# A two-block transformer on one core: five of eight modulation loads move from the ring to GpSimd's queue, and two orders in the expert mixtures change

## The reference

```
def first_block(x, c, ada_w, ada_b, norm1_g, norm2_g, even_w_in, even_w_out, ...):
    c_act = jax.nn.silu(c)
    for layer in range(DEPTH):
        mod = (c_act @ ada_w[layer] + ada_b[layer])[:, None, :]
        sh1, sc1, g1, sh2, sc2, g2 = jnp.split(mod, 6, axis=-1)
        h = rms_norm(x, norm1_g[layer]) * (1.0 + sc1) + sh1
        if layer % 2 == 0:
            mix = even_mixer(h, even_w_in[i], even_w_out[i], ...)
        else:
            mix = odd_mixer(h, odd_w_in[i], odd_w_out[i])
        x = x + g1 * mix
        h = rms_norm(x, norm2_g[layer]) * (1.0 + sc2) + sh2
        x = x + g2 * grouped_moe(h, router_w, router_b, exp_w_gate[layer], exp_w_up[layer], exp_w_down[layer])
    return x
```

## Time and profile before

| | us |
|---|---|
| median of 3 runs | 2006.47 |
| lowest, highest | 2000.43, 2013.55 |
| the profiled execution | 2012.27 |
| its span | 2010.2 |
| TensorE busy in it | 1887.3 |
| VectorE busy | 1182.9 |
| ScalarE busy | 944.8 |

### The profile page before, as it was taken

The page is one execution under the profiler, slowest core; times in us unless marked ns, Lnnn a source line. Parts: engine busy times, 40 slices in busy tenths (PEclk is TensorE's granted clock), DMA queues, the critical chain, the costliest instruction groups (busy, mean ns, idle before and its releaser), DMA issues.

```text
span 2010.2 us, 32548 instructions
## 1 busy us (share of the span) xinstructions
PE 1887.3 (94%) x13756; PEld 1388.2 (69%) x13756; DVE 1182.9 (59%) x1634; ACT 944.8 (47%) x1346; POOL 72.2 (4%) x126
## 2 busy tenths in 40 slices
PE   7988998899988988999999999899999999899998
PEld 4776623246975342358889877788888888778887
DVE  5878733446877433556666744666665676536665
ACT  3445444446463544464446633354455454545443
POOL 1040000000110000000000000000000000200000
PEclk9989997999998979999999989999999999999999
DMA  9876899997956899975555200345545555505552
GB/s 372 331 250 256 332 416 390 421 421 282 343 159 278 356 388 421 420 296 202 189 189 178 92 24 4 146 170 189 188 160 203 193 188 189 153 19 192 189 189 105
DMA packets 69216, 476.42 MB, mean 237 GB/s; under 512 B 8512, under 2 KB 8576, under 8 KB 13776
## 3 DMA queue, kind: packets, MB, share of 16 engines
q1 hardware_dynamic: 60592, 437.32, 57.0%
q0 software_dynamic: 8480, 37.03, 5.6%
HBM read 472.17 MB, written 2.14 MB: 236 GB/s over the span
## 4 chain that ended last, share of the span: by engine, by line
PE 74%; DMA 9%; DVE 9%; ACT 5%; issue 3%; SPq 0%; POOL 0%; DVEq 0%; ACTq 0%; POOLq 0%
PE psum L1160 16%; PE psum L1195 11%; PE psum L1608 11%; PE psum L1165 8%; DMA experts<-in_exp_blocks 6%; PE psum L1115 4%; PE psum L1550 1%; DVE w_lo L3102 1%; PE psum L1128 1%; PE psum L1623 1%; PE psum L1129 1%; PE psum L1130 1%; DMA pool<-in_ada_w 1%; ACT w_hi L2331 1%; PE psum L1064 1%
## 5 line engine op out<-in xcount | busy, mean ns | idle before, releaser
L3102 DVE TENSOR_TENSOR w_lo<-ring,w_hi 128x2048 fp32r<-128x2048 f32 x191 | 436.9, 2293 | 183.9 <-ACT w_hi L2331 182.4
L2331 ACT ACTIVATE w_hi<-ring 128x2048 fp32r<-128x2048 f32 x191 | 365.1, 1915 | 203.6 <-PE psum L1195 117.9
L1160 PE MATMUL psum<-h_both,w_hi 128*128 128x512 f32 x1408 | 442.5, 395 | 1.9 <-DVE h_both L3888 1.3
L1165 PEld LDWEIGHTS psum<-h_both,w_lo 128*128 128x128 f32 x1408 | 264.5, 188 | 61.8
L1165 PE MATMUL psum<-h_both,w_lo 128*128 128x256 f32 x1408 | 277.2, 278 | 0.0
L2540 ACT ACTIVATE pool<-experts 128x512 f32 x332 | 183.8, 622 | 186.2 <-PE psum L1608 115.5
L3546 DVE COPY pool<-experts 128x512 f32 x380 | 141.4, 423 | 201.9 <-PE psum L1608 129.1
L1160 PEld LDWEIGHTS psum<-h_both,w_hi 128*128 128x128 f32 x1408 | 217.3, 189 | 5.7 <-issue 1.7
L2363 ACT ACTIVATE pool<-psum 128x512 f32<-128x512 f32 x88 | 52.7, 598 | 254.3 <-PE psum L1165 254.3
L1608 PE MATMUL psum<-pool 128*32 128x512 f32 x1008 | 123.2, 604 | 12.9 <-DVE pool L3546 11.5
L1608 PE MATMUL psum<-experts,pool 128*32 128x512 f32 x1024 | 122.5, 613 | 3.7 <-DMA experts<-in_exp_blocks 1.9
(11 more groups left out here) (508 smaller groups left out, 3004.3 us busy)
## 6 DMA issues: line engine op xcount, KB each, us to landing
ring<-in_weight_pieces SPq DMA_DIRECT2D x193, 1024.0 KB, 4.8
experts<-in_exp_blocks SPq DMA_DIRECT2D x192, 1024.0 KB, 15.4
ring<-in_ada_w SPq DMA_DIRECT2D x24, 1024.0 KB, 6.0
pool<-in_ada_w POOLq DMA_DIRECT2D x16, 1024.0 KB, 8.9
pool<-in_ada_w POOLq DMA_DIRECT2D x16, 512.0 KB, 4.5
pool<-bias_rows POOLq DMA_DIRECT2D x20, 128.0 KB, 4.2
pool<-in_mem_w_blocks SPq DMA_DIRECT2D x2, 1024.0 KB, 10.2
experts<-in_mem_w_blocks SPq DMA_DIRECT2D x2, 1024.0 KB, 11.4
```

What stands on the lines that cost most here:

```text
L1160: pe.matmul(bank(4 + 2 * j + f).rearrange("p (s n) -> p s n", s=2), wh[:, k, P * f:P * f + P], h_both[:, :, k, :], start=k == 0, stop=Fals ...
L1165: return pe.matmul(bank(4 + 2 * j + f)[:, 0:T], wl[:, k, P * f:P * f + P], h_hi[:, k, :], start=False, stop=k == KD - 1, skip_group_check= ...
L2331: act.activation(w_hi[:, (s["split"] + r) % 3, :], piece(s["pieces"][r]), ACT.Copy)\
L3102: dve.tensor_tensor(w_lo[:, slot, :], piece(s["pieces"][r]), w_hi[:, slot, :].bitcast(F32), ALU.subtract).then_inc(sem("w_lo"), 1)
```

## The change

First, the modulation rows 0 to 4 of the second third leave the ring. GpSimd's queue loads them one after another into two idle regions, `XN` (odd rows) and `HT` (even rows). `side_load(row)` waits for the landing of the one before (the first: for the five small tables, on the same semaphore, now named `tables_in`), and from row 2 on for VectorE to have used row - 2. Rows 0 and 1 are issued ahead of `c_even`, row 2 behind it, rows 3 and 4 behind the stores of the bias rows and ahead of the row of `ada_b`. VectorE uses them after weight pieces 2, 3, 4, 6 and 7 (`side_ada`). Rows 5, 6 and 7 stay in the ring, behind pieces 9, 11 and 13. Second, in both mixtures ScalarE takes the silu of groups 0 to 3 in pass 7 after its copies for groups 6 and 7. Third, in the second mixture the columns 4 to 7 of the first half are scaled after the copies of pass 0 rather than before.

```
-EVEN_ADA = [None, None] + [(row, 1) for row in range(6)] + [None, (6, 1), (7, 1), None, None, None] + [(row, 2) for row in range(8)]
+EVEN_ADA = [None] * 9 + [(5, 1), None, (6, 1), None, (7, 1)] + [(row, 2) for row in range(8)]
+SIDE_ADA = {2: 0, 3: 1, 4: 2, 6: 3, 7: 4}
...
+        def side_in(row):
+
+            return view(XN if row % 2 else HT, PIECE)
...
             pl.wait_ge(sem("h_split_lo"), SPLIT_BASE["n_even"] + SPLITS["n_even"])
+            ada_0 = a["ada_w"][0].rearrange("(p t) n -> p (t n)", t=KD)
+
+            def side_load(row):
+
+                at = PIECE * (ADA_PER_ROW * row + 1)
+                if row:
+                    pl.wait_ge(sem("tables_in"), 80 + 16 * row)
+                else:
+                    pl.wait_ge(sem("tables_in"), 80)
+                if row in (2, 3):
+                    pl.wait_ge(sem("ada_used"), KD + row - 1)
+                elif row == 4:
+                    pl.wait_ge(sem("ada_used"), KD + 3)
+                pl.dma_start(side_in(row), ada_0[:, at:at + PIECE]).then_inc(sem("tables_in"), 16)
+
+            side_load(0)
+            side_load(1)
             pl.dma_start(view(WORK, 2176), a["c_even"]).then_inc(sem("even_in"), 16)
+            side_load(2)
             pl.wait_ge(sem("bias_rows"), 2)
             pl.dma_start(scratch_bias[0:8, :], view(WORK + 4256, 512)[0:8, :]).then_inc(sem("even_in"), 16)
             pl.dma_start(scratch_bias[8:20, :], view(WORK + 4768, 512)[0:12, :]).then_inc(sem("even_in"), 16)
+            side_load(3)
+            side_load(4)
             pl.wait_ge(sem("even_in"), 48)
             pl.dma_start(ada_rows[0], a["ada_b"][0:1, 2 * D:3 * D]).then_inc(sem("ada_b_in"), 16)
...
                 if c == 3:
                     act.wait_ge(sem("cols_in"), 64)
-                    act.wait_ge(sem("ada_used"), KD + 6)
+                    act.wait_ge(sem("ada_used"), KD + 5)
...
-                for k in range(0, KD, 2):
+                for k in range(0, 4 if layer else KD, 2):
                     gathered(k, 0)
...
                 if layer:
                     for g in range(BASE_GROUPS, GROUPS):
                         copied(0, g)
+                    for k in range(4, KD, 2):
+                        gathered(k, 0)
...
                     copied(p, 4)
                     copied(p, 5)
-                    for g in range(4):
-                        if p == 7:
-                            silu(g)
                     if p in (19, 23):
                         y_high(p, 3)
                     copied(p, 6)
                     copied(p, 7)
                     if p == 7:
+                        for g in range(4):
+                            silu(g)
...
-                if nm == "even_in" and EVEN_ADA[n]:
-                    ada_piece(KD + n - (n > 8) - 2)
+                if nm == "even_in" and n in SIDE_ADA:
+                    side_ada(SIDE_ADA[n])
+                elif nm == "even_in" and EVEN_ADA[n]:
+                    ada_piece(KD + EVEN_ADA[n][0])
...
+            def side_ada(row):
+
+                dve.wait_ge(sem("tables_in"), 96 + 16 * row)
+                dve.wait_ge(sem("ada_used"), KD + row)
+                if row == 0:
+                    dve.tensor_scalar(acc_0[1], side_in(0), csilu[:, 0:1], None, ALU.mult).then_inc(sem("ada_used"), 1)
+                else:
+                    dve.scalar_tensor_tensor(out=acc_0[1], in0=side_in(row), scalar=csilu[:, row:row + 1], in1=acc_0[1],
+                                             op0=ALU.mult, op1=ALU.add).then_inc(sem("ada_used"), 1)
```

More of the change, by code:

```diff
@@ L172, in ada @@
         self.ada_order.append((len(self.pieces), row, third))
-        self.add("ada", ADA_PER_ROW * row + third, ("ada_used", len(self.ada_order)))
+        self.add("ada", ADA_PER_ROW * row + third, ("ada_used", KD * third + row + 1))
     def gemm(self, name, width, deep=KD, feat=(), between=()):
@@ L841, in _ @@
             hot = view(WORK + 2176, 4, 512)
-            pl.dma_start(hot[:, 0:2, :], a["c_hot_rel"].rearrange("(k p) n -> p k n", p=P)).then_inc(sem("hot_in"), 16)
-            pl.dma_start(hot[0:32, 2, :], a["c_hot_t5"]).then_inc(sem("hot_in"), 16)
-            pl.dma_start(hot[0:12, 3, :], a["c_ban"]).then_inc(sem("hot_in"), 16)
-            pl.dma_start(view(WORK + 4224, 2, 8), a["rel_t"].rearrange("(k p) n -> p k n", p=P)).then_inc(sem("hot_in"), 16)
-            pl.dma_start(view(WORK + 4240, 12)[0:32, :], a["rel_bias_2"]).then_inc(sem("hot_in"), 16)
-            pl.wait_ge(sem("h_split_lo"), SPLIT_BASE["n_even"] + SPLITS["n_even"])
+            pl.dma_start(hot[:, 0:2, :], a["c_hot_rel"].rearrange("(k p) n -> p k n", p=P)).then_inc(sem("tables_in"), 16)
+            pl.dma_start(hot[0:32, 2, :], a["c_hot_t5"]).then_inc(sem("tables_in"), 16)
+            pl.dma_start(hot[0:12, 3, :], a["c_ban"]).then_inc(sem("tables_in"), 16)
+            pl.dma_start(view(WORK + 4224, 2, 8), a["rel_t"].rearrange("(k p) n -> p k n", p=P)).then_inc(sem("tables_in"), 16)
+            pl.dma_start(view(WORK + 4240, 12)[0:32, :], a["rel_bias_2"]).then_inc(sem("tables_in"), 16)
+            pl.wait_ge(sem("h_split_lo"), SPLIT_BASE["n_even"] + SPLITS["n_even"])
+            ada_0 = a["ada_w"][0].rearrange("(p t) n -> p (t n)", t=KD)
[12 more added lines that the diff above has]
+            side_load(1)
             pl.dma_start(view(WORK, 2176), a["c_even"]).then_inc(sem("even_in"), 16)
+            side_load(2)
             pl.wait_ge(sem("bias_rows"), 2)
@@ L1339, in bias_products @@
                     pe.wait_ge(sem("cols_in"), 64)
-                    pe.wait_ge(sem("hot_in"), 80)
+                    pe.wait_ge(sem("tables_in"), 80)
                     hot = view(WORK + 2176, 4, 512)
@@ L3199, in ada_piece @@
             def ada_piece(n):
-                no, row, third = PL.ada_order[n]
+                no, row, third = PL.ada_order[n if n < KD else n - len(SIDE_ADA)]
                 dve.wait_ge(sem(f"landed{PL.pieces[no]['slot']}"), PL.pieces[no]["landed"])
@@ L3281, in even_first @@
                     dve.wait_ge(sem("bias_ps"), 2)
-                    dve.wait_ge(sem("hot_in"), 80)
+                    dve.wait_ge(sem("tables_in"), 80)
                     dve.tensor_copy(view(WORK + 4256, 512)[0:8, :], bank(4)[0:8, :]).then_inc(sem("bias_rows"), 1)
@@ L3291, in even_first @@
                 if c == 2:
-                    bias_row(0, KD + 5)
+                    bias_row(0, KD + 4)
                     for e in moved("even_in", 1):
@@ L3508, in gathered @@
                         ada_part(n)
-                for k in range(1, KD, 2):
+                for k in range(1, 4 if layer else KD, 2):
                     gathered(k, 0)
@@ L3580, in moe @@
                         copied(0, g)
+                    for k in range(5, KD, 2):
+                        gathered(k, 0)
                 for k in range(1, KD, 2):
```

## The result

The changed kernel takes 2014.93 us, median of 14 runs (2011.66 to 2019.00); the kernel before, in its 14 runs beside them, 2006.15 (2000.06 to 2013.55). The ratio is 1.0043, 95% interval 1.0031 to 1.0055: 8.6 us slower, from 6.2 to 11. The forecast was 1.5 us faster.

A forecast was written before the change was run, and what follows sets the result against it. TensorE was taken to hold 74% of the chain of waits, with the expert-block stream setting the mixtures' end. Projection +6, mixtures -7.6 and gathered columns nothing gave -1.6 us on the 2006.47 median: 2005, range 1991 to 2016.

The forecast's parts named there:

- the rival with costs and no gains: Whole kernel: projection costs +9, mixtures give 0 to 1 as the dry stretch only moves; 2015 us, chance 0.15.
- the durations of the side-load chain: First projection, GpSimd's queue: side loads landing at 64.3, 69.3, 77.3 and 87.4, the `ada_b` row at 94.
- The stall before piece 4: First projection: bias rows made at 81, TensorE wanting them at 78.8, a stall of about 2 us.
- The low part of piece 7: First projection: VectorE, waiting for the `ada_b` row, ends it at 101.7 in place of 94.1; bias reads 7.6 us later.
- What comes back at piece 10: First projection: piece 11's load 3.7 us sooner against the bias reads, so piece 10 starts 3.9 us later than 119.1.
- The decayed scores: End of the first projection: they come some 6 us later, and TensorE then runs slowly for about 2.
- my upper bound of +9: First projection: sum of costs and returns from +4 to +9 us, with +6 taken.
- The cover for the moved piece: First projection: VectorE's 2.62 us wait for ScalarE covers the last modulation piece (2.35), moved behind piece 13's low part.
- The mixtures: -7.6: Both mixtures: silus behind the copies start pass 8 sooner and close the dry stretch, 3.8 us gained in each.
- the third rival: Mixtures: TensorE, not the expert stream, sets their end; about 8 us gained in each, total 1996, chance 0.1.
- the dry stretch: Both mixtures, behind pass 8: 3.2 and 3.5 us of ten without transfers, expected to close with the new silu order.
- The gathered columns: Second mixture, pass 0: loads go out 1.5 us sooner but the next wait for TensorE; nothing, between -1 and +1.

The follow-up runs named there:

- proj_only: The changed kernel with both mixtures' orders as in the kernel before, so only the first projection changed; 2015.44 us, ratio 1.0054 to the kernel before.
- late2: The changed kernel with VectorE using side row 2 after weight piece 5 in place of 4; 2009.28 us, ratio 1.0023 to the kernel before.
- row_first: The changed kernel with the row of `ada_b` issued ahead of the fourth and fifth side loads; 2013.05 us, ratio 1.0031 to the kernel before.
- late3: row_first with VectorE using side rows 2, 3 and 4 after weight pieces 5, 7 and 8; 2007.74 us, ratio 0.9999 to the kernel before.
- late3_silu: late3 with the second mixture's gathered columns in their old order, silus still behind the copies; 2006.70 us, ratio 1.0002 to the kernel before.
- late4: late3_silu with two modulation pieces moved behind the decayed scores; 2003.06 us, ratio 0.9985 to the kernel before.
- late4_again: late4 unchanged, run once more for a second trace; 1999.69 us in one run.
- silu_only: The kernel before with only the four silus of pass 7 moved behind the copies of groups 6 and 7, both mixtures; 2000.94 us, ratio 0.9985.
- gather_only: The kernel before with only the second mixture's gathered columns 4 to 7 moved behind the first copies; 2006.53 us, ratio 1.0003.
- control: The kernel before, unchanged, run once more for a second trace; 2010.57 us in one run.
- tail_silu: silu_only with the first modulation piece of the last third moved behind the decayed scores, no side loads; 1998.63 us, ratio 0.9967 to the kernel before.

## Why the prediction was wrong

The time was 2014.9 for a forecast of 2005.0. The forecast had the change 1.5 us faster, and it is 8.6 us slower. That lies inside the range up to 2016 and at the rival with costs and no gains (2015, chance 0.15), but its number fits in part by luck: that rival adds 9 for the projection and takes off 1 for the mixtures, where proj_only shows 10.8 (7.0 to 14.8) for the projection and the traces 12.6 and 13.0.

**The step that failed first: the durations of the side-load chain.** The order of events was as put, each link late. The forecast had the first three loads landed at 64.3, 69.3 and 77.3, the bias rows at 81, the row at 94 and the low part of piece 7 at 101.7; they came at 66.5, 73.3, 80.9, 84.4, 100.7 and 108.2. The loads took 8.54, 6.52, 7.30 and 5.09 us for 7.1, 5.0, 8.0 and 5.4, and the row 9.04 us where I had put 6. The first two loads and the row, 1.4, 1.5 and 3.0 us too long, make most of the 6.5 us. I had counted ring loads beside the first and the third load, but none beside the row: the two that go out at 87.33 and 89.53 are released by the low parts of pieces 5 and 6, which come in one go after VectorE's late start at 85.01. The fifth side load, issued behind both at 91.10, took 9.40 us; the fourth, issued ahead of them at 85.73, took 5.09. A late chain so brings its own company. The Trainium skill (DMA: Bandwidth & Descriptors, "Issuing engines are not separate DMA queues") says that transfers of all issuing engines interleave on the same 16 DMA engines; these durations of one and the same megabyte agree.

**The stall before piece 4** was put at 2 us and was 5.68 and 6.90 in the two traces of after (2.06 in proj_only), and I gave no price to the lower clock behind it: the shift is 8.4, 5.7 of it idle and 2.7 clock. late2 shows the whole part by taking it away (0).

**The low part of piece 7** came 14.1 us late, not 7.6, and VectorE had stood 7.50 us before the row. row_first and late2 show that it is not the row alone: the fourth side load or the fifth binds next.

**What comes back at piece 10** held. Counted as in the forecast, from the low part of piece 7 (14.1 late) to the restart (10.1 late), it is 4.0 us for 3.7; the 7.0 of the table takes in before's slow clock there. The restart is 10.1 us later than before's and not 3.9 because the chain ahead of it is late by that much more. **The decayed scores**: TensorE began behind them 10.8 us later, for 6. Sum +12.6 and +13.0, beyond my upper bound of +9, for which the prediction gives no terms. Its middle doesn't add up either: 6 for the scores and 2 for the slow clock behind them are 8, and +6 was taken.

**The cover for the moved piece.** I let VectorE's wait of 2.62 us cover it. When the head statistics come later there is no such wait (in after VectorE goes from them to the low part of piece 13 at 141.21 without one): late3 and late3_silu lose 6.7 and 7.0 us at the end of the projection, late4 and late4_again, with two pieces taken out of the way, -0.4 and +0.4. That both moved pieces were needed isn't shown.

**The mixtures: -7.6 was mis-sized; silu_only shows 3.0 together (6.2 to -0.4), gather_only nothing.** That the stream matters more than TensorE's early start was right: the third rival's 8 us a mixture came in no run. But I read the dry stretch of the earlier trace rows as the work of the 3.34 us of idle time, and it comes only where the clock also stays low for long behind that wait. By the traces' clock records TensorE had 0.50 for 20 us in both mixtures of before (DMA share 0.68 and 0.65 behind), for 17 in the second of control (0.77), for some 14 in the first of control (0.97), and for 3 to 10 in the two mixtures of proj_only and of gather_only, where no window behind pass 8 is under 1.01. These are executions as they fell, not an experiment on the clock; with the new order the low stretch is 10 us at most in ten traces, and none is dry. With the old silus, the stream is 216.3, 216.3 and 216.5 us in three other traces of the first mixture and, in the second, 217.5 in proj_only but 219.3 in control, where the clock stayed low; with the new ones 216.1 to 216.9 and 217.2 to 218.0 (old gathered order). Only in the executions in which the clock stays low is there something to gain in the stream, up to 2.9 us a mixture (219.2 to 216.3, 220.4 to 217.5). The shift of -4.0 and -2.9 between the two profiles measured for the most part before's bad luck: with the old silus the same stages are 2.6 us shorter than before's in proj_only, gather_only and control, and 3.1, 3.1 and 1.1. In seven of the ten traces with the new silus the first is 3.9 to 4.0 shorter, in the others 2.1 to 3.0; so a gain of some 1 us there, beside the stream, isn't excluded, and no run explains it. The rival said that the dry stretch would come again in the new profile; it did not, and there was no gain all the same.

The Trainium skill (TensorE: Matmul & The Clock Gate, "HAM oscillation") has a wait of a few microseconds send the engine to half clock. A stretch at 0.50 followed each of the eight waits of 3.34 us in the traces with the old silus, as the page has it, and yet the wait's price can't be read off it. In three mixtures (both of before, the second of control) it lasted 17 to 20 us without a break, in the other five 3 to 14 us in all, and twice it began only some 5 us behind the wait: in the second mixture of proj_only 1.00 was granted up to 730 and 0.83 in the next ten microseconds, where before had 0.50 and 0.53. And with a wait of only 0.31 us, in the new order, nine of ten traces of the first mixture still have 3 to 10 us at 0.50 there, two of the second mixture too (late3, tail_silu). The prediction took before's length for the wait's price; the sum should have been made for a short and for a long stretch.

**The gathered columns** were put at nothing, and gather_only's trace shows the reason given: loads sooner out, and then a dry place before the stream goes on.

What stays open: how often the clock stays low in pass 7, and why there, since each kernel has one trace or two; the size of the silus' gain (6.2 us to none); and where tail_silu's 6.6 us come from.

## What to carry to other kernels

When loads move to a second queue, draw the chain of landings against the in-order engine that uses them, and put each use behind work that the engine has anyway; here a load that landed 3.6 us later than forecast held up every later step of VectorE, and then the ring that waits for it. Look for small transfers and small steps (a bias row, a copy out of PSUM) behind the moved ones. Never size a gain by an idle gap of one execution: compare at least two traces of the unchanged kernel, instruction by instruction, and see whether the gap is in both.

## What was not expected of the hardware

The same 3.34 us wait of TensorE, in the same place of the second mixture, was followed by 20 us at a granted clock of 0.50 in before, and in proj_only by 1.00 for the next 5 us and 0.50 for 3 us after them. A stage that nobody touched (1120 to 1310) is 6.9 us apart between two executions, at least 4 of it where one of them ran at 0.80 to 0.86 for 30 us. And a 4 KB row issued 0.5 us behind a 1 MB load on the same queue took 9.04 us, landing 0.2 us behind it (100.67 and 100.50), and so in the three other traces with that order (7.1 to 9.0 us, 0.2 us behind); behind two small stores it took 2.3 to 4.6 (late3_silu, row_first).
